# Shift and scale of the first norm as rows on TensorE, and c loaded ahead of x

## The reference

```
sc = silu(c)                                  # c: 1024 values
mod = sc @ ada_w + ada_b                      # 9 vectors of 1024
(sh1, sc1, g1, ...) = split(mod, 9)
y = rmsnorm(x, ffn1_pre_g) * (1.0 + sc1) + sh1
y = swiglu(y, w_gate, w_up, w_down)           # width 2816
```

## Time and profile before

| | |
|---|---|
| median of three runs | 2391.21 us |
| profiled execution | 2391.95 us |
| its span | 2390.2 us |
| PE (TensorE) busy | 2331.9 us, 98% |
| DVE (VectorE) busy | 1329.6 us, 56% |
| ACT (ScalarE) busy | 826.7 us, 35% |
| POOL (GpSimd) busy | 206.5 us, 9% |

### The profile page before, as it was taken

The page is one execution under the profiler, slowest core; times in us unless marked ns, Lnnn a source line. Parts: engine busy times, 40 slices in busy tenths (PEclk is TensorE's granted clock), DMA queues, the critical chain, the costliest instruction groups (busy, mean ns, idle before and its releaser), DMA issues.

```text
span 2390.2 us, 26549 instructions
## 1 busy us (share of the span) xinstructions
PE 2331.9 (98%) x10706; PEld 1902.5 (80%) x10706; DVE 1329.6 (56%) x1916; ACT 826.7 (35%) x1226; POOL 206.5 (9%) x170
## 2 busy tenths in 40 slices
PE   8999999999999999999999999999999989999998
PEld 6888888877788888888788888888767767888887
DVE  7655548486238455547543466664456664644343
ACT  3322223324324322223633342322334443433221
POOL 0000004021014000003110100000121111000001
PEclk8999999999999999999999999999999999999999
DMA  8765632311112356531331246663121112443330
GB/s 314 245 204 201 198 120 78 106 42 39 62 54 71 106 201 209 198 124 44 112 98 56 80 139 221 208 211 119 58 95 55 54 45 71 126 130 97 97 97 35
DMA packets 80792, 287.99 MB, mean 120 GB/s; under 512 B 8976, under 2 KB 9104, under 8 KB 80672
## 3 DMA queue, kind: packets, MB, share of 16 engines
q1 hardware_dynamic: 79952, 284.74, 36.3%
q10 hardware_dynamic: 720, 1.57, 0.2%
HBM read 284.18 MB, written 2.10 MB: 120 GB/s over the span
## 4 chain that ended last, share of the span: by engine, by line
PE 87%; DVE 7%; ACT 3%; issue 1%; DMA 0%; POOL 0%; SPq 0%; DVEq 0%; ACTq 0%; POOLq 0%
PE bank L273 23%; PE bank L274 22%; PE bank L275 22%; PE bank L337 2%; PE bank L338 2%; PE bank L342 2%; DVE wlo L1388 2%; PE bank L384 2%; PE bank L316 1%; PE bank L317 1%; PE bank L318 1%; PE bank L428 1%; ACT whi L867 1%; DVE attd L1699 1%; PE bank L520 1%
## 5 line engine op out<-in xcount | busy, mean ns | idle before, releaser
L1388 DVE TENSOR_TENSOR wlo<-raw,whi 128x1024 fp32r<-128x1024 f32 (+1 forms) x370 | 477.3, 1291 | 387.8 <-ACT whi L867 387.5
L273 PE MATMUL bank<-yhi,whi 128*128 128x512 f32 x1632 | 647.4, 397 | 4.5 <-DVE wlo L1388 3.7
L275 PE MATMUL bank<-yhi,wlo 128*128 128x512 f32 x1632 | 637.3, 391 | 0.0
L274 PE MATMUL bank<-ylo,whi 128*128 128x512 f32 x1632 | 637.3, 390 | 0.0
L867 ACT ACTIVATE whi<-raw 128x1024 fp32r<-128x1024 f32 (+1 forms) x370 | 385.3, 1042 | 325.9 <-PE bank L275 247.4
L273 PEld LDWEIGHTS bank<-yhi,whi 128*128 128x128 f32 x1632 | 307.3, 188 | 87.0 <-issue 21.2
L275 PEld LDWEIGHTS bank<-yhi,wlo 128*128 128x128 f32 x1632 | 307.5, 188 | 65.4
L274 PEld LDWEIGHTS bank<-ylo,whi 128*128 128x128 f32 x1632 | 307.7, 189 | 61.6 <-issue 0.7
L275 PE MATMUL bank<-mlp_ahi,wlo 128*128 128x512 f32 x512 | 199.2, 389 | 0.0
L274 PE MATMUL bank<-mlp_alo,whi 128*128 128x512 f32 x512 | 199.2, 389 | 0.0
L273 PE MATMUL bank<-mlp_ahi,whi 128*128 128x512 f32 x512 | 199.2, 389 | 0.0
(11 more groups left out here) (321 smaller groups left out, 2794.0 us busy)
## 6 DMA issues: line engine op xcount, KB each, us to landing
raw<-in_ada SPq DMA_DIRECT2D x152, 512.0 KB, 4.3
raw<-in_ffn_up SPq DMA_DIRECT2D x88, 512.0 KB, 4.3
raw<-in_mlp_up SPq DMA_DIRECT2D x64, 512.0 KB, 3.6
raw<-in_mlp_dn SPq DMA_DIRECT2D x64, 512.0 KB, 3.6
raw<-in_ffn_dn SPq DMA_DIRECT2D x32, 512.0 KB, 3.7
raw<-in_w_dqkv SPq DMA_DIRECT2D x24, 512.0 KB, 3.6
first<-in_ada SPq DMA_DIRECT2D x16, 512.0 KB, 15.1
raw<-in_ffn_dn SPq DMA_DIRECT2D x16, 384.0 KB, 3.5
```

The lines of the kernel that those rows point to most:

```text
L273: e.matmul(out, wh, xh, start=first, stop=False)
L274: e.matmul(out, wh, xl, start=False, stop=False)
L275: mm = e.matmul(out, wl, xh, start=False, stop=last)
L1388: e.tensor_tensor(k.wlo[:, what % NW, 0:width], raw[:, 0:width], k.f(k.whi[:, what % NW, 0:width]), ALU.subtract).then_inc(*sig.up("wlo", ...
```

## The change

The eight tiles of `sh1` and `sc1` are now made on TensorE but for tile 0 of each, which stays on VectorE. `shift` goes. In its place stand `first_rows` and `first_columns` on TensorE and `first_row` on ScalarE. For tile n, `first_rows` does 16 matmuls (two vectors, eight kt): the stationary operand is one column of silu(c) repeated 32 times (128 x 32), the 128 x 128 matrix block moves, and the output goes to one of four groups of 32 partitions of a bank (kt mod 4). ScalarE copies the result (128 x 256) to SBUF, and `first_columns` turns it into columns by two matmuls with one moving column of the constant 1/32, which sums the four groups. Tile 1 comes ahead of the first network; tile n + 1 comes in step n of `four`: the rows ahead of the products of units 0 and 1, the columns between them and those of units 2 and 3.

VectorE reads both vectors from the bank and no longer does ten of its twelve multiplies; the splits of units 2 and 3 stand one tile earlier. c is loaded ahead of SyncE's tiles of x, and ScalarE's Silu of c and the load of the root's table stand ahead of the squares. The bytes loaded stay the same; units 2 and 3 stand after tiles 2 and 3 of the modulation matrix (before: 3 and 4).

```diff
-    def shift(self, n):
+    def first_rows(self, n):
-        out = k.banks.at("shift", n % 3) if n > 3 else self.bank("shift", n % 3, hold=True)
-        if n > 3:
-            w.wait_ge(*sig.on("mod0", n - 3))
+        out = k.banks.at("rows")
         w.wait_ge(k.s_first[n], 32)
         w.wait_ge(*sig.on("sil"))
-        for kt in range(8):
-            mm = self.e.matmul(out[:, n:n + 1], k.first_ada[0][n][:, 128 * kt:128 * kt + 128], k.sil[:, kt:kt + 1],
-                               start=kt == 0, stop=kt == 7)
+        if n > 2:
+            w.wait_ge(*sig.on("row", n - 2))
+        for v in range(2):
+            c = slice(256 * (n % 2) + 128 * v, 256 * (n % 2) + 128 * v + 128)
+            for kt in range(8):
+                q = slice(32 * (kt % 4), 32 * (kt % 4) + 32)
+                mm = self.e.matmul(out[q, c], k.sil[:, kt:kt + 1].to_broadcast([128, 32]),
+                                   k.first_ada[v][n][:, 128 * kt:128 * kt + 128], start=kt < 4, stop=kt >= 4)
+        mm.then_inc(*sig.up("rows", n))
+
+    def first_columns(self, n):
+        out = k.banks.at("vec")
+        w.wait_ge(*sig.on("row", n))
+        for v in range(2):
+            mm = self.e.matmul(out[:, 8 * v + n:8 * v + n + 1], k.first_row[:, n % 2, v, :],
+                               k.cst[:, PART_C:PART_C + 1], start=True, stop=True)
         mm.then_inc(*sig.up("vec", n))
...
+    def rows_ahead(self, n):
+        if 1 <= n < NT - 1:
+            self.first_rows(n + 1)
+    def columns_ahead(self, n):
+        if 1 <= n < NT - 1:
+            self.first_columns(n + 1)
...
-        for n in SHIFTS[0:2]:
-            self.shift(n)
+        self.first_rows(1)
+        self.first_columns(1)
...
         for n in range(NT):
-            self.prep_to((0, 1, 1, 2, 3, 3, 3, 3)[n])
+            self.prep_to((0, 1, 2, 3, 3, 3, 3, 3)[n])
+            if n == 0:
+                self.first_row(1)
...
+            if 1 <= n < NT - 1:
+                self.first_row(n + 1)
+    def first_row(self, n):
+        k, half = self.k, 256 * (n % 2)
+        self.w.wait_ge(*self.sig.on("rows", n))
+        if n > 2:
+            self.w.wait_ge(*self.sig.on("vec", n - 2))
+        self.e.activation(k.first_row[:, n % 2, :, :].rearrange("p v f -> p (v f)"),
+                          k.banks.at("rows")[:, half:half + 256], k.ACT.Copy)
...
+        w.wait_ge(k.s_c, 16)
+        e.activation(k.crow[:, :], k.crow[:, :], k.ACT.Silu).then_inc(*sig.up("crow", 0))
+        self.ready_root()
         for n in range(NT):
             w.wait_ge(k.s_tile[n], 16)
-            if n == 7:
...
             self.square("sq", ("start", n), k.tm(n)[:, 0:S], k.h[:, n, :])
...
         self.ada(1, 0)
         self.ada(0, 0)
-        self.ada(1, 1)
...
-            w.wait_ge(*sig.on("ada", 1, n))
+            if n:
+                w.wait_ge(*sig.on("vec", n))
...
             if n == 0:
                 self.prep_to(0)
-            if n + 2 not in SHIFTS and n + 2 < NT:
-                self.ada(0, n + 2)
             low(n)
-            if n + 2 < NT:
-                self.ada(1, n + 2)
-            if n < 4:
-                self.prep_to((1, 1, 2, 3)[n])
+            if n < 3:
+                self.prep_to((1, 2, 3)[n])
...
+        e.dma_start(k.crow[:, :], k.dram["c"]).then_inc(k.s_c, 16)
         for n in range(1, NT, 2):
             e.dma_start(k.h[:, n, :], k.dram["x"][:, n, :]).then_inc(k.s_tile[n], 16)
-        e.dma_start(k.crow[:, :], k.dram["c"]).then_inc(k.s_c, 16)
```

More of the change, by code:

```diff
@@ L24 @@
 PI_A, PI_B, PI_C = 6.28125, 2029 / 2**20, 2 * math.pi - 6.28125 - 2029 / 2**20
-SHIFTS = range(1, 5)
 INV_FREQ = np.power(np.float32(500000.0), -np.arange(0, 16, 2, dtype=np.float32) / np.float32(16)).astype(np.float32)
@@ L34 @@
 ]
-IDENT, ONES, PERM, CAUS, CNEG, INVF_C, EPS_C, HPI_C, SEL_C, NCONST = 0, 128, 256, 384, 512, 640, 641, 642, 643, 647
+IDENT, ONES, PERM, CAUS, CNEG, INVF_C, EPS_C, HPI_C, SEL_C, PART_C, NCONST = 0, 128, 256, 384, 512, 640, 641, 642, 643, 647, 648
 MIX_ORDER = [("mif", 0, 1), ("hq", 0, 4), ("hf", 0, 4), ("hi", 0, 4)]
@@ L68, in constants @@
     c[:, HPI_C] = math.pi / 2
+    c[:, PART_C] = 1 / 32
     for h in range(4):
@@ L321, in tokens, with four @@
             mm.then_inc(*sig.up("lin", u))
-    def four(self, tags, x, hi, lag=0, before=None):
+    def four(self, tags, x, hi, lag=0, before=None, between=None):
         w, sig, e, k = self.w, self.sig, self.e, self.k
@@ L350, in four @@
             for kt, group in ((n, us[0:2]), (n - lag, us[2:4])) if lag else ((n, us),):
+                if between and group[0] > us[0]:
+                    between(n)
                 if not 0 <= kt < NT:
@@ L448, in up @@
                 done = 4
[L449 to L452, removed]
+                if st == "ffn1":
+                    self.four([tag] * 4, y, "yhi", 3, self.rows_ahead, self.columns_ahead)
+                    k.banks.let_go(("rows",))
+                    k.banks.let_go(("vec",))
+                else:
+                    self.four([tag] * 4, y, "yhi", 0 if st == "ffn2" else 3)
             for _ in range(done, n):
@@ L469, in ffn @@
             self.totals_end(st)
-    def shift_ahead(self, n):
-        if n + 2 in SHIFTS[2:]:
-            self.shift(n + 2)
+    def rows_ahead(self, n):
[4 more added lines that the diff above has]
+            self.first_columns(n + 1)
     def decay(self, st, q, kk, bg):
@@ L834, in program @@
         self.root("start", 0)
-        for n in SHIFTS[0:2]:
-            self.shift(n)
+        self.bank("rows", hold=True)
+        self.bank("vec", hold=True)
+        self.first_rows(1)
+        self.first_columns(1)
         self.ffn("ffn1", FFN_GROUPS, True)
@@ L963, in first_norm @@
                               bias=k.mod[:, n:n + 1]).then_inc(*sig.up("yhi", "ffn1", n))
+            if 1 <= n < NT - 1:
[6 more added lines that the diff above has]
+        self.e.activation(k.first_row[:, n % 2, :, :].rearrange("p v f -> p (v f)"),
+                          k.banks.at("rows")[:, half:half + 256], k.ACT.Copy).then_inc(
+            *self.sig.up("row", n, bank=("rows",) if n == 7 else None))
     def ffn(self, st, counts, gated):
@@ L1500, in low @@
                                    ALU.subtract).then_inc(*sig.up("ylo", "ffn1", n))
+        vec = k.banks.at("vec")
         for n in range(NT):
             w.wait_ge(*sig.on("bias1"))
-            w.wait_ge(*sig.on("ada", 1, n))
[L1505 to L1511, removed]
+            if n:
+                w.wait_ge(*sig.on("vec", n))
+            else:
+                w.wait_ge(*sig.on("ada", 1, 0))
+                w.wait_ge(*sig.on("ada", 0, 0))
+            e.scalar_tensor_tensor(A[:, n:n + 1], vec[:, 8 + n:9 + n] if n else k.mod[:, 8:9], one[:, n:n + 1],
+                                   g[:, n:n + 1], ALU.add, ALU.mult).then_inc(*sig.up("coef", "ffn1", n))
+            e.tensor_tensor(k.mod[:, n:n + 1], vec[:, n:n + 1] if n else k.mod[:, 0:1], k.pc("ada_b", n),
+                            ALU.add).then_inc(*sig.up("mod0", n, bank=("vec",) if n == 7 else None))
             w.wait_ge(*sig.on("spread", "R", "start"))
@@ L2159, in program @@
         e.dma_start(k.cst[:, :], k.dram["cst"]).then_inc(k.s_cst, 16)
+        e.dma_start(k.crow[:, :], k.dram["c"]).then_inc(k.s_c, 16)
         for n in range(1, NT, 2):
             e.dma_start(k.h[:, n, :], k.dram["x"][:, n, :]).then_inc(k.s_tile[n], 16)
-        e.dma_start(k.crow[:, :], k.dram["c"]).then_inc(k.s_c, 16)
         for n in range(NT):
[L2164 to L2167, removed]
+            for v in (1, 0):
+                src = k.dram["ada_0"][v, n - 1] if n else k.dram["ada"][v, 0]
+                e.dma_start(k.first_ada[v][n], src).then_inc(k.s_first[n], 16)
+            for u in ((), (0, 1), (2,), (3,), (), (), (), ())[n]:
                 e.dma_start(k.raw[:, u, :], k.dram["ffn1_up0"][u]).then_inc(k.s_raw[u], 16)
@@ L2250, in build_program @@
             k.first_ada = [[first[:, v, n, :] for n in range(NT)] for v in range(2)]
+            k.first_row = sb("first_row", [128, 2, 2, 128], fp32, s)
         hidden("ffn1", FFN_GROUPS)
@@ L2389, in lay_out @@
     w = x["ada_w"][0]
-    d["ada_0"] = by_feature(w[:, 128 * SHIFTS[0]:128 * SHIFTS[-1] + 128])
+    d["ada_0"] = np.stack([by_feature(w[:, 1024 * v + 128:1024 * v + 1024]) for v in range(2)])
     d["ada"] = w.T.reshape(9, 8, 128, 1024)
```

4 lines of the change are left out of this document (1 added, 3 removed).

## The result

The changed kernel takes 2394.84 us (median of 22 runs) against 2391.56 us for the kernel before on the same chips (22 runs): +3.3 us, ratio 1.0014 with a 95% interval of 1.0008 to 1.0021. It is slower by 0.14%, which is inside the 0.2% that the prediction called no change. The forecast was +3.0 us. The time was met; the way to it was not, as the trace shows.

What follows compares the result with a forecast made beforehand. TensorE was taken as the bound. Start 20.5 + products 21.8 + columns 3.0 + rows 13.2 + half clock 2.3 + waits 3.9 = 64.7, taken as 63.6 against 60.56: +3.0 us, 2394.2 us; range 2387 to 2407.

Steps and rivals of the forecast that it cites:

- 96 products at full clock: First stage, TensorE: 96 matmuls of 512 columns at 0.227 us each, 21.8 us.
- rows of seven tiles, full clock: TensorE, tiles 1 to 7: 224 passes, 1.9 us a tile with neighbouring groups overlapping in pairs, 13.2 us.
- columns: TensorE, after each tile's copy: 28 passes of one moving column at 0.107 us, 3.0 us.
- half clock: TensorE from near 20 us: clock falls, returns by about 27 us; costs 2.3 us.
- waits: TensorE waits for tile 1's copy, unit 1's wlo, the chain in steps 1 and 2, and the last tile: 3.9 us.
- overlap taken off: First stage: some waits fall where the clock is slow and hide, so about 1 us comes off.
- A1, A2+B1, B2+C1, ...: Rows on TensorE: a matmul's second pass overlaps the next one's first; 17 pass times for 32 passes, 1.9 us a tile.
- rival 1: Rows on TensorE: four groups at once, 6.2 us of rows, waits 5.8, total 2389.4 us; chance 0.25.
- The head: Before the first rows: squares end later, VectorE does one multiply less; net 0.2 us earlier, rows start at 20.5.
- The loads and VectorE cost nothing: First stage: last tile's load lands near 37.5 us, before TensorE needs it; VectorE stays level with TensorE; no cost.
- the late clock: TensorE stays at half clock until 40 us or later, costing 10 instead of 2.3 us, total 2401; chance 0.12.
- the case given 0.40: Rows overlapping in pairs with the clock back early: 2391 to 2397 us, likeliest 2394.2; chance 0.40.

Runs made afterwards that it cites:

- the run with the old head: Changed kernel with c loaded behind SyncE's tiles of x and Silu and table load between squares 6 and 7, as before; ratio 0.9998 to the kernel before.
- the combined versions: Changed kernel with old load and ScalarE order plus two constant matmuls in TensorE's head waits, then further edits added one by one; ratios 0.9991, 0.9993, 0.9988, 0.9968.
- the two tiles ahead: Rows, copy and columns made two tiles ahead, not one: on the changed kernel alone ratio 1.0005; added to old head and two constant matmuls 0.9993.
- the early split: Unit 1's weight split moved ahead of tile 1's copy and tile 0's ylo, added to old head, constant matmuls and two tiles ahead; ratio 0.9988.
- the loads in the order of need: Weight units 2 and 3 loaded behind matrix tiles 4 and 5 and split one step later, added to the version with unit 1 split early; ratio 0.9968.
- its head filled: One more constant matmul ahead of the partition sums and one between sums and spread: on the kernel before ratio 0.9994, on the changed kernel 0.9999.

## Why the prediction was right in time and wrong in its steps

| step | predicted | in the trace |
|---|---|---|
| rows of tile 1 start | 20.5 | 21.81 |
| 96 products at full clock | 21.8 | 21.8 |
| rows of seven tiles, full clock | 13.2 | 7 x 1.01 = 7.1 |
| columns | 3.0 | 7 x 0.37 = 2.6 |
| half clock | 2.3 | (11.0 - 1.8) / 2 = 4.6 |
| waits | 3.9 | 4.6 |
| first products and gaps at a switch | none | 1.8 |
| overlap taken off | -1 | - |
| start of linear | 63.6 | 64.3 summed, 63.83 read |

- **TensorE bounds the stage:** right for the kernel before. In the changed one it waits 4.6 us there (0.7, 0.94, 0.13, 1.0, 1.3 and 0.5, from the end of one instruction's share to the start of the next).
- **The rows:** wrong, and the largest error. "A1, A2+B1, B2+C1, ...", two passes at a time, was my order; the trace and four runs show four groups at once, rival 1, in both orders that were run. 13.2 us in place of 7.1, 6 us too much.
- **The head:** wrong in sign. I forecast it 0.2 us earlier. I followed the squares and forgot that the seven adds behind them are a chain of 5.5 us that had been hidden by the arrival of x. Holding the first square back to 10.66 uncovers it. 1.3 us too little for the start of the rows; by the run with the old head 1.8 us of head in all.
- **The clock:** right that it falls and returns sooner than before; it returned at 32.8 and not at 27 us. 2.3 us too little.
- **The waits:** right in kind and nearly in size (`yhi` in steps 2 and 3, `wlo` of unit 1, the copy of tile 1, the last tile), though with rows four at once the same reasoning gave 5.8.
- **Not in the sum:** behind rows, columns or a wait the second product starts 0.34 or 0.31 us after the first and not 0.227 (43.28 to 43.62, 45.14 to 45.45, 55.98 to 56.32), and a gap of up to 0.1 us stands ahead of most of the rows: about 14 x 0.1 + 4 x 0.1 = 1.8 us. The first part is not the price of another tile shape: it stands behind a mere wait too, and in the run without groups, where all stationary operands are 128 x 128, it is 0.31 us behind the rows (52.04 to 52.35). The gap ahead of the rows is missing in that run.
- **The loads and VectorE cost nothing:** right here; with the other waits gone they become the bound, as the combined versions show.

- **Slips in the arithmetic:** rows 7.0 less and waits 1.9 more make rival 1 5.1 less and not 4.9, and the late clock costs 10 - 2.3 = 7.7 us on top of the forecast, which is +10.7 and not +10 (with four groups at once +5.9 and not +5). The 1.15 us of a multiply, ascribed to rows 5, is the distance between two starts; the row's mean is 1.218. None of this moves the forecast.

So errors of 1.3, 2.3, 0.7 and 1.8 us in one direction stood against 6.1 and 0.4 us in the other. That they nearly cancel is luck: the case given 0.40 did not happen. The case that came true is rival 1, given 0.25, to which I had put 2389.4 us; with its head and clock as measured it lands where I had put another case. What did the change bring? The rows on TensorE run four groups at once. The gain from them went to the later head (shown: 1.8 us), to the clock lost in the head's wait (3.8 us in one trace, 2.4 to 3.6 over all runs, with intervals that touch), and to waits in a chain one tile long (shown in the trace; what it is worth by itself is not settled by the medians). That the span grew by 2.3 us (2390.2 to 2392.5) where linear moved by 3.3 lies in the part behind, 2329.6 and 2328.7 us long; 1 us is little beside the 8 us by which that part differs among the runs.

## What to carry to other kernels

Before one moves a load or a Silu ahead of a chain, look at what the arrival of the data had been hiding behind it: here seven adds. An engine's wait in the head can cost more through the clock than through its own length, and filling it with work that nobody needs is the cheapest edit of this study. And when a stage is bound by one engine with others close behind, edits pay together: head and clock gave 5 us of linear, the two tiles ahead and the early split next to nothing, and with the loads in the order of need as well 2.9 us (58.86 to 55.98). Before one puts such a gain down to the edit, look at the clock of both traces: that of two tiles ahead by itself can be all the clock's.

## What the runs showed of the hardware that was not expected

- Float32 matmuls with 128 x 32 stationary and 128 moving columns: 0.110, 0.054 and 0.026 us a pass with one, two and four groups of output partitions, with nearly the same time (1.08 and 1.12 us for 32) whether two or four passes of one group follow each other.
- In the kernel before with its head filled, the clock fell to 0.50 from a full clock 1.7 us into 32 one-column passes back to back. In the changed kernel with its head filled it stayed at 1.00 to 40 us, with TensorE busy 7.96 and 7.46 us of 10.
- Behind a wait or behind other work on TensorE, the second 512-column product starts 0.31 to 0.34 us after the first at full clock, in place of 0.227, with or without a change of the stationary operand's shape.
